# A decoder step with paged attention: ten cache slots instead of eight, another order of softmax work and convolution taps

## What is computed

```python
x  = LN(alpha*x + gate0 * 0.5 * SwiGLU_1(mod0(x)))
q, k, v, ga, gb = split(mod1(x) @ w_in)              # 8 heads of 64, convolution of 512 channels
attn = MoBA(q, k, v, cache_k, cache_v, page_table)   # new tokens: 2048 cached keys in 8 blocks, top 3 blocks
conv = silu(groupnorm(depthwise_conv31(ga * sigmoid(gb))))
x  = LN(alpha*x + gate1 * concat(attn*beta_attn, conv*beta_conv) @ w_out)
x  = LN(alpha*x + gate2 * 0.5 * SwiGLU_2(mod2(x)))
```

## Time and profile before

| | us |
|---|---|
| median of 3 runs (lowest, highest) | 899.49 (899.29, 901.28) |
| the profiled execution | 899.64 |
| its span, first to last instruction | 897.9 |
| TensorE busy | 841.3 (94%) |
| VectorE busy | 457.7 (51%) |
| ScalarE busy | 351.1 (39%) |
| GpSimd busy | 266.8 (30%) |

### The profile page before, as it was taken

One profiled execution on the slowest core, in us unless ns is written; L12 is line 12 of the kernel. 1 busy time (PEld: TensorE's weight loads), 2 busy tenths in 40 slices (PEclk: granted clock), 3 DMA queues, 4 the chain that ended last, 5 costly groups with the idle time before them and its releaser, 6 DMA issues.

```text
span 897.9 us, 17144 instructions
## 1 busy us (share of the span) xinstructions
PE 841.3 (94%) x6798; PEld 745.1 (83%) x6798; DVE 457.7 (51%) x710; ACT 351.1 (39%) x502; POOL 266.8 (30%) x326
## 2 busy tenths in 40 slices
PE   5899999999999999999997779769999999999996
PEld 3789889898899989988764556538899999999996
DVE  1543434343334576745686776844864444444454
ACT  2332333333222467445352314273573333332240
POOL 2020000000010323999999999700200000000121
PEclk9999999999999999999999899999999999999998
DMA  9977777789857444417997999999524444643421
GB/s 300 349 235 255 231 247 243 225 268 303 289 183 244 147 146 145 138 54 236 359 304 269 355 339 362 348 348 290 158 77 153 147 140 141 195 146 134 160 76 58
DMA packets 182130, 197.44 MB, mean 220 GB/s; under 512 B 11908, under 2 KB 163706, under 8 KB 182054
## 3 DMA queue, kind: packets, MB, share of 16 engines
q1 hardware_dynamic: 175149, 190.04, 65.2%
q10 hardware_dynamic: 6624, 6.33, 2.2%
q0 software_dynamic: 288, 0.14, 0.1%
HBM read 193.67 MB, written 3.17 MB: 219 GB/s over the span
## 4 chain that ended last, share of the span: by engine, by line
PE 75%; DVE 8%; SPq 6%; DMA 5%; ACT 3%; issue 3%; POOL 1%; DVEq 0%; ACTq 0%; POOLq 0%
PE bank L1620 19%; PE bank L1621 18%; PE bank L1622 18%; PE bank L1909 5%; SPq L446 3%; PE bank L1587 3%; PE bank L1934 2%; DMA raw<-in_w_ada 2%; DMA raw<-in_ffn_wg 1%; PE bank L1576 1%; DVE kT L1383 1%; PE bank L1652 1%; DMA raw<-in_ffn_wu 1%; DVE wlo L1094 1%; PE bank L1646 1%
## 5 line engine op out<-in xcount | busy, mean ns | idle before, releaser
L1094 DVE TENSOR_TENSOR wlo<-raw,whi 128x2048 fp32r<-128x2048 f32 (+1 forms) x80 | 182.8, 2286 | 235.5 <-ACT whi L716 235.2
L1620 PE MATMUL bank<-mh,whi 128*128 128x320 f32 x816 | 257.5, 316 | 0.0
L1622 PE MATMUL bank<-mh,wlo 128*128 128x320 f32 x816 | 252.2, 309 | 0.0
L1621 PE MATMUL bank<-ml,whi 128*128 128x320 f32 x816 | 252.2, 309 | 0.0
L716 ACT CAST whi<-raw 128x2048 fp32r<-128x2048 f32 (+1 forms) x80 | 148.9, 1861 | 229.3 <-PE bank L1622 155.0
L1620 PEld LDWEIGHTS bank<-mh,whi 128*128 128x128 f32 x816 | 153.3, 188 | 10.4 <-issue 10.3
L1621 PEld LDWEIGHTS bank<-ml,whi 128*128 128x128 f32 x816 | 153.5, 188 | 0.1
L1622 PEld LDWEIGHTS bank<-mh,wlo 128*128 128x128 f32 x816 | 153.3, 188 | 0.0
L1620 PE MATMUL bank<-hh,whi 128*128 128x320 f32 x352 | 111.1, 316 | 0.0
L1621 PE MATMUL bank<-hl,whi 128*128 128x320 f32 x352 | 109.6, 311 | 0.0
L1622 PE MATMUL bank<-hh,wlo 128*128 128x320 f32 x352 | 109.4, 311 | 0.0
(11 more groups left out here) (280 smaller groups left out, 1134.3 us busy)
## 6 DMA issues: line engine op xcount, KB each, us to landing
araw<-in_w_ada SPq DMA_DIRECT2D x28, 1024.0 KB, 5.2
raw<-in_ffn_wg SPq DMA_DIRECT2D x22, 1024.0 KB, 7.1
raw<-in_ffn_wu SPq DMA_DIRECT2D x22, 1024.0 KB, 7.5
raw<-in_ffn_wd SPq DMA_DIRECT2D x16, 1024.0 KB, 5.0
raw<-in_cache_k SPq DMA_DIRECT2D x64, 256.0 KB, 4.5
raw<-in_cache_v SPq DMA_DIRECT2D x60, 256.0 KB, 5.7
raw<-in_w_in SPq DMA_DIRECT2D x10, 1024.0 KB, 5.2
raw<-in_w_ada SPq DMA_DIRECT2D x8, 1024.0 KB, 11.9
```

The costliest lines, as they stand in the source:

```text
L1094: dve.tensor_tensor(wl(slot_w(phase, u))[:, 0:size], landed(phase, u)[:, 0:size], wh(slot_w(phase, u))[:, 0:size].bitcast(F32), ALU.subtra ...
L1620: pe.matmul(bank[:, b, 0:T], wh(slot)[:, c], h_, start=(start and n == 0), stop=False)
L1621: pe.matmul(bank[:, b, 0:T], wh(slot)[:, c], l_, start=False, stop=False)
L1622: ins = pe.matmul(bank[:, b, 0:T], wl(slot)[:, c], h_, start=False, stop=(stop and n == len(parts) - 1))
```

## The change

Parts: (1) ten slots instead of eight, the two new ones, kvm and kvu, laid over mh and over the first chunks of uT; the last fourteen units have a table of their own, KV_LAST, which leaves slots 6 and 7 (kvw) free for W_out after pair 3's keys. Waits are added for what reads mh and uT before, and one before mh is written. uT's chunks are renumbered (v in 4 to 7, k in 8 to 11), so that k stays out of the way. (2) The order of the softmax steps on TensorE and VectorE. (3) The taps: chunk 0's are spread, and six of chunk 3's go from GpSimd to VectorE. (4) ScalarE issues its pages earlier. The diff, cut; first_taps replaces conv_taps where that was called for chunk 0, and blocks_added returns its last instruction:

```diff
@@ -114 @@
 ADA0 = 8
-KVN, KV_RING = 64, 8
+KVN, KV_RING = 64, 10
+KV_LAST = (0, 1, 2, 3, 4, 5, 8, 9, 0, 1, 4, 5, 2, 3)
 ACT_HIGH = (8 + 2, 8 + 5)
+THIRD = 6
@@ -177 @@
 def kv_slot(kvi):
...
-    return kvi % KV_RING if kvi < KVN - 8 else (0, 1, 2, 3, 4, 5, 2, 3)[kvi - KVN + 8]
+    return kvi % KV_RING if kvi < KVN - len(KV_LAST) else KV_LAST[kvi - KVN + len(KV_LAST)]
...
 def kv_turn(kvi):
@@ -256 @@
 yT = sb("yT", [P, NCH, T])
+with ExitStack() as scope:
+    kvm = sb("kvm", [P, UMAX], F32, scope)
@@ -289 @@
     yrow = sb("yrow", [P, 3, D], F32, scope)
+with ExitStack() as scope:
+    kvu = sb("kvu", [P, UMAX], F32, scope)
@@ -344 @@
 def kv_raw(kvi):
...
     k = kv_slot(kvi)
+    if k >= 8:
+        return (kvm, kvu)[k - 8][:, :]
...
 def kT_view(k, half):
@@ -360 @@
 ld_c, c_t, ld_ident = sem("ld_c"), sem("c_t"), sem("ld_ident")
+own_moved, gate_moved, third_prompt, third_sample = sem("own_moved"), sem("gate_moved"), sem("third_prompt"), sem("third_sample")
@@ -564 @@
         sp.wait_ge(w_lo, WIN[0] + WIN[2] - RING + kvi + 1)
+    elif kvi < 9:
+        sp.wait_ge(w_used, WIN[0] + (7, 7, 10, 9, 10)[kvi - RING])
     else:
-        sp.wait_ge(w_used, WIN[0] + (7, 7, 10, 9)[kvi - RING])
+        sp.wait_ge(ps_mm, NH)
+        sp.wait_ge(tok_t, 8)
+        sp.wait_ge(q_ready, 1)
     load_pages(sp, cache, kvi, numbers[8 * (k % 4 // 2) + k % 2:], range(3 if cache == "v" and j < 3 else 4))
-    if kvi == KV_RING + 3:
+    if kvi == KV_RING + 4:
...
         sp.dma_start(o["conv_prompt_new"][0, 0], cout).then_inc(stored_early, 16)
-    if kvi == 4 * KV_RING:
+    if kvi == 32:
...
         for u in range(2):
-            sp.wait_ge(v_used, 16 + 7 + u)
+            sp.wait_ge(kt_ready, 2 * (24 + 7 + u))
...
 for u in range(2, WOUT[2]):
-    load(WOUT, u, cols(i["w_out"], slice(UC * u, UC * u + UC)), NCH * UC, (v_used, 24 + u - 1))
+    load(WOUT, u, cols(i["w_out"], slice(UC * u, UC * u + UC)), NCH * UC, (v_used, 24 + u + 1))
@@ -676 @@
 sam = cbuf[:, c, ST + SEQ:CB].rearrange("p (b k) -> p b k", b=DB)
-for k in range(TAPS):
+if c == 3:
+    pool.wait_ge(third_prompt, THIRD)
+    pool.wait_ge(third_sample, THIRD)
+for k in range(THIRD if c == 3 else 0, TAPS):
@@ -924 @@
 elif c < 12:
-    act.copy(uT[:, c, :], src).then_inc(u_out, 1)
+    act.copy(uT[:, c + 4 if c < 8 else c - 4, :], src).then_inc(u_out, 1)
@@ -970 @@
 def last_page(k, page):
...
     kvi = values_at(j - 1, k)
-    act.wait_ge(kt_ready, 2 * (8 * j + k + 1))
+    cache_b, jb, kb = kv_chunk(kv_before(kvi))
+    act.wait_ge(*((kt_ready, 2 * (8 * jb + kb + 1)) if cache_b == "k" else (v_used, 8 * jb + kb + 1)))
...
     n = 8 * j + k
-    if j and k % 4 == 1:
-        numbers = page_numbers(2 * (j - 1) + k // 4, mybir.EngineType.Activation)
@@ -986 @@
             act.copy(kT_view(k, 1), bank_keys(1)).then_inc(kt_high, 1)
-        if j and k:
-            last_page(k - 1, numbers)
+        if j and k in (0, 3):
+            numbers = page_numbers(2 * (j - 1) + k // 3, mybir.EngineType.Activation)
+        if j and k == 0:
+            last_page(0, numbers)
+        if j and k < 7:
+            last_page(k + 1, numbers)
...
             between[k]()
-    if j:
-        last_page(7, numbers)
...
 def probs(j):
...
-    act.wait_ge(eb_ready, j + 1)
...
     for b2 in range(2):
+        act.wait_ge(eb_ready, 2 * j + b2 + 1)
@@ -1054 @@
 act.wait_ge(gy_ready, c + 1)
+act.wait_ge(v_used, 24 + 1)
@@ -1301 @@
-def conv_taps(first, last):
+def conv_taps(c, first, last, on_prompt, on_sample):
...
+def first_taps(first, last):
+    conv_taps(0, first, last, conv_prompt, conv_sample)
@@ -1365 @@
 sbk, sc = bank[:, 4 + g % 2, :], s_two[j % 2][:, b2, P * n:P * n + 512]
-dve.tensor_reduce(gsum[:, j % 2, b2, n:n + 4], sbk.rearrange("p (m x) -> p x m", x=4), AX, ALU.add)
+ins = dve.tensor_reduce(gsum[:, j % 2, b2, n:n + 4], sbk.rearrange("p (m x) -> p x m", x=4), AX, ALU.add)
+if g == 3:
+    ins.then_inc(gsum_ready, 1)
@@ -1393 @@
                                 con[:, C_OWN + 56 - DT * (2 * j + b2):C_OWN + 56 - DT * (2 * j + b2) + NS], ALU.add)
-    ins.then_inc(gsum_ready, 1)
+    ins.then_inc(own_moved, 1)
...
 def blocks_chosen(j):
...
     s, top = s_two[j % 2], bmax[:, j % 2]
-    dve.wait_ge(gsum_ready, j + 1)
+    dve.wait_ge(own_moved, j + 1)
...
     link(dve.tensor_copy(gate[:, :, :], bank[:, 6, 256:272].rearrange("p (b n) -> p b n", b=2)))
-    dve.tensor_reduce(top[:, 0:1, 8:9], s[:, 0:1, PAST // 2:], AX, ALU.max)
+    dve.tensor_reduce(top[:, 0:1, 8:9], s[:, 0:1, PAST // 2:], AX, ALU.max).then_inc(gate_moved, 1)
@@ -1439 @@
 def first_pair():
...
+    own_added(0)
     score_chunk(0, 3)
-    own_added(0)
...
 def first_bias():
...
-    blocks_added(0, 1)
     bias_ready(0)
+    blocks_added(0, 1).then_inc(eb_ready, 1)
...
 keys_high(0, {0: lambda: prompt_probs(7)})
-keys_high(1, {0: first_pair, 1: lambda: blocks_chosen(0), 3: lambda: blocks_added(0, 0), 4: first_bias, 7: lambda: sums_ready(0)})
-taps = (12, 12, 25, TAPS)
+keys_high(1, {0: first_pair, 1: lambda: blocks_chosen(0), 3: lambda: blocks_added(0, 0), 4: first_bias, 6: lambda: own_added(1), 7: lambda: sums_ready(0)})
...
     if j > 1:
-        keys_high(j)
+        between = {6: lambda: own_added(j)}
+        if j == 2:
+            for n, k in enumerate((1, 3, 5, 7)):
+                between[k] = lambda n=n: first_taps(17 + n, 18 + n)
+        keys_high(j, between)
     score_chunk(j, 3)
-    own_added(j)
     blocks_chosen(j)
-    for b2 in range(2):
-        blocks_added(j, b2)
+    blocks_added(j, 0)
     bias_ready(j)
-    if j == 3:
+    blocks_added(j, 1).then_inc(eb_ready, 1)
+    if j < 3:
+        first_taps(*((12, 17), (21, 25))[j - 1])
+    else:
...
     sums_ready(j)
-    if j < 3:
-        conv_taps(taps[j], taps[j + 1])
+    if j == 1:
+        dve.wait_ge(glu_ready, NCC)
+        conv_taps(3, 0, THIRD, third_prompt, third_sample)
+    if j == 2:
+        first_taps(25, TAPS)
@@ -1812 @@
 def turn_tokens(e):
...
-    at = (8, 4)[e % 2] + 2 * (e // 2)
+    at = (4, 8)[e % 2] + 2 * (e // 2)
@@ -1846 @@
     pe.wait_ge(ps_ready, h)
-q, k = uT[r, h // 2, :], uT[r, 4 + h // 2, :]
+q, k = uT[r, h // 2, :], uT[r, 8 + h // 2, :]
@@ -1937 @@
 def own_scores(j):
...
     pe.wait_ge(gl_out, 2)
+    if j == 1:
+        pe.wait_ge(eb_ready, 1)
...
             ins = pe.matmul(bank[QG * g4:QG * g4 + QG, 6, NS * b2:NS * b2 + NS], qo[:, 2 * j + b2, g4, :],
-                            uT[:, NHP + g4, SEQ:T], start=True, stop=True)
+                            uT[:, 8 + g4, SEQ:T], start=True, stop=True)
...
 def pair_keys(j, between={}):
@@ -1951 @@
     scores(j, k - 1)
-if k == 4 and j != 1:
+if k == (5 if j == 1 else 4):
@@ -1969 @@
 def prob_sum(j):
+    if j == 0:
+        pe.wait_ge(own_moved, 2)
...
 def pair_probs(j):
@@ -1984 @@
 pe.wait_ge(ri_ready, j + 1)
+if j == 0:
+    pe.wait_ge(gate_moved, 2)
@@ -1997 @@
 raw_wait(kvi)
+if k % 2 == 0:
+    pe.wait_ge(pt_evac, 5 * j + k // 2 + 1)
@@ -2009 @@
+pe.wait_ge(pt_evac, 5 * j + 5)
@@ -2030 @@
 pair_keys(0, {0: lambda: prompt_steps(20), 1: lambda: prompt_steps(21), 2: lambda: prompt_steps(22), 3: turn_glu})
-pair_keys(1, {1: lambda: gate_sum(0), 3: lambda: max_swap(0), 6: lambda: prob_sum(0)})
+pair_keys(1, {1: lambda: gate_sum(0), 3: lambda: max_swap(0), 7: lambda: prob_sum(0)})
+gate_sum(1)
 pair_probs(0)
-pe.wait_ge(pt_evac, 5)
-own_scores(1)
...
 def next_pair(j):
...
         pair_keys(j)
-        pe.wait_ge(pt_evac, 5 * j)
-    steps = {0: lambda: gate_sum(j), 2: lambda: max_swap(j), 5: lambda: prob_sum(j)}
+    steps = {4: lambda: max_swap(j), 7: lambda: prob_sum(j)}
+    if j > 1:
+        steps[0] = lambda: gate_sum(j)
     if j == 3:
-        steps[3] = group_means
+        steps[6] = group_means
@@ -2071 @@
-pe.wait_ge(pt_evac, 20)
...
 def conv_half(u, c0, c1):
```

More of the change, by code:

```diff
@@ L1298, in _ @@
             half_gate(2)
-            def conv_taps(first, last):
-                sum_c = yT[:, NCC, :]
+            def conv_taps(c, first, last, on_prompt, on_sample):
+                sum_c = yT[:, NCC + c, :]
                 for k in range(first, last):
-                    sam = cbuf[:, 0, ST + SEQ:CB].rearrange("p (b k) -> p b k", b=DB)[:, :, k:k + DT]
-                    w = dwT[:, NCC * k:NCC * k + 1]
+                    sam = cbuf[:, c, ST + SEQ:CB].rearrange("p (b k) -> p b k", b=DB)[:, :, k:k + DT]
+                    w = dwT[:, NCC * k + c:NCC * k + c + 1]
                     if k == 0:
                         dve.wait_ge(x_ready, 8)
-                        dve.tensor_scalar(sum_c[:, 0:SEQ], cbuf[:, 0, k:k + SEQ], w, par2[:, 0:1], ALU.mult, ALU.add).then_inc(conv_prompt, 1)
-                        dve.tensor_scalar(samples(sum_c), sam, w, par2[:, 0:1], ALU.mult, ALU.add).then_inc(conv_sample, 1)
-                    else:
-                        dve.wait_ge(conv_prompt, k)
-                        dve.scalar_tensor_tensor(sum_c[:, 0:SEQ], cbuf[:, 0, k:k + SEQ], w, sum_c[:, 0:SEQ], ALU.mult, ALU.add).then_inc(conv_prompt, 1)
```

(16 more changed lines are left out.)

## The result

The median went from 900.07 us (899.29 to 901.28, 4 runs) to **894.34 us** (893.76 to 895.61, 4 runs): a ratio of 0.9943, 95% interval 0.9924 to 0.9961, so 5.7 us of gain where 10.4 were forecast. The time lies in the range, at its upper edge. The profiled execution took 895.61 us, its span 893.7.

The account below looks back on a forecast made before the run. The DMA engines' page stream was taken as the bound: 12.9 us missing, less 2.0 emptiness and 0.5 stores, net 10.4. 899.64 - 10.4 - 0.15 = 889.1, stated as 889.0 us; range 884.5 to 894.5.

Parts of the forecast that it names:

- pages bound the stage and the gain is the stream's: Attention stage: the DMA engines' page stream sets the end; filling its short stretches gains 10.4 us net.
- units 24 and 25 out by 476: Pair 0's values: these units go into slots 4 and 5 and issue from 475.6 instead of 482.1 us.
- the readers' schedule: TensorE's attention stages: pair 2's keys at 493.1, pair 1's values at 520.6, pair 2's at 562, pair 3's at 579 us.
- C: Rival, chance 0.06: VectorE becomes the bound, 21 taps among pairs 1 and 2 adding up to 12 us to readers; 896.
- D: Rival, chance 0.04: slower, as with more pages in flight the engines move less after 476 us; 905 in all.
- What stays: Of 12.9 us missing in the stream, 2.0 of emptiness near 481 us and 0.5 for convolution-state stores remain; net 10.4.
- 345 GB/s or more in each stretch from 482 to 595: Sign that the forecast is right: page rate in the attention stage; under 330 with a SyncE wait would show it wrong.
- what stands behind the sixth page follows at a fixed distance: After the last pair's sixth value page: W_out products, last turn and FFN 2 move as a block with unit 61.
- bounded the clock by 0 and 2: TensorE's longer idling before unit 60 could put up to 2 us more work at 1.2 GHz; taken as 0.
- On the path all this costs or gives nothing: New softmax order and taps: covered by the stream; without that cover worth 11 us by pair 2's earlier values.
- not the bound: SyncE's queue from 475.6 us: 115 us of issues, the last could go at 591; engines land that unit near 601.
- GpSimd's last tap: GpSimd loses 6 of 93 taps at 2.26 us and ends near 565 instead of 578.9 us.

Follow-up runs that it names:

- The slot series: Nine, ten and eleven page slots with the new softmax order and taps, beside the kernel before: 897.4, 894.7 and 892.4 us.
- clock_kept: Changed kernel plus twelve matmuls of unused constants on TensorE ahead of value unit 60: 892.94 us, ratio 0.9945 to the kernel before.
- after_again: The changed kernel itself, unchanged, run again beside other versions on one chip: 894.72 us, ratio 0.9947 to the kernel before.
- eleven_slots: Changed kernel with an eleventh slot laid over xT, so the output is not the reference's: 892.40 us, ratio 0.9925 to the kernel before.
- quarters_late: Changed kernel, ScalarE issuing the last pair's fourth value pages, units 60 to 63's behind the group norm's square root: 892.30 us, ratio 0.9931 to the kernel before.
- act_quarters: Changed kernel, ScalarE issuing the last pair's fourth value pages, units 60 to 63's ahead of the group norm's square root: 892.88 us, ratio 0.9927 to the kernel before.
- quarters_late_clock: quarters_late plus six products of constants on TensorE before value unit 60: 893.24 us, ratio 0.9923 to the kernel before.

## Why the prediction was right and wrong

**Right, with numbers:** that pages bound the stage and the gain is the stream's (8.39 us of waiting before unit 60); units 24 and 25 out by 476; the readers' schedule, within 1.2 us up to pair 2's values; no TensorE wait over 1.3 us for a key copy (against C); no loss of rate with more pages in flight, 352 for values and 374 to 385 for keys in the full stretches (against D). Pair 3's values came at 582.6 instead of 579: TensorE waited four times, 3.7 us in all, for pages of pair 2, and ran the eight products of group_means in 3.23 us instead of 2.42, at a granted clock of 0.73.

**The step that failed is "What stays".** I let 2.0 us of emptiness and 0.5 for the stores remain of 12.9. By the same formula on the stretches after: 476-482 70 x 6 / 380 = 1.1; 482-500 54 x 18 / 380 = 2.6; 528-548 6 x 20 / 380 = 0.3; 573-592 27 x 19 / 348 = 1.5: **5.5 us** remain. The edge at 482 cuts through the dry stretch, so by its own edges: the dry stretch, to 483.5, cost 2.6 us where I had left 2.0, and the 4.5 us at part of the rate behind it 1.0 where I had left none. With what little is missing beside them that is 3.7 at the seam, and 3.9 and 3.8 in the two other profiles of the changed kernel. The other miss is a stretch that had been full before, 573 to 592 at 347 GB/s (1.5, none allowed; 1.0 and 0.3 in the other two). I had counted the loss of 482 to 500 as the hole's and took it to go with the hole. That loss goes with a wait at that seam, and the wait stayed: with eleven slots and no dry stretch it is still 336 GB/s. By my own signs, "345 GB/s or more in each stretch from 482 to 595" failed twice, at 326 and 321. So 12.9 - 5.5 = 7.4 were to come; unit 61 came 6.3 us earlier, with the stage starting 0.6 us later in this execution (the prompt's last turning products but one at 419.57, before at 418.96).

The simpler count was at hand in my own text: unit 26 waits for pair 0's first values, "at 481 too". Before it was unit 24. From that wait's end on, two units fewer have to cross: 2 x 2.8 = 5.6 us, and the distance fell by 6.4. By this count emptiness **ahead** of a wait that stays is no gain beyond the units that the new slots take across in it; the 2.8 us of 450 to 476 and the 1.5 of 426 to 450 brought pages forward to stand before the same wait. The slot series fits (2.5 us each, 5.2 from eight to ten with the new readers); that the gain follows this count and no other is argued, not shown.

**A second step failed: "what stands behind the sixth page follows at a fixed distance".** It was 291.4 us before and 293.5 after. I had bounded the clock by 0 and 2 and took 0, "since part of it was slow before"; it cost 1.2. Before, the clock was full to 602 us, with TensorE idle from 599 to 603.4, and four W_out products ran slowly (0.41 to 0.64 us instead of 0.31, until 609.5); now TensorE idled from 588.8 to 597.2, the clock was at the lower level, 1.2 GHz, from about 592 on, and thirteen products, to 605.7, ran slowly. The Trainium skill (TensorE: Matmul & The Clock Gate, "What's actually happening") has idleness bring the lower clock back, the rule that I had weighed; the trace agrees. Of the other 0.9 us nearly all, 0.75, lies in the last 11 us of the kernel, from ScalarE's last activation to the end: 10.2 us before, 10.9 after. ScalarE and the products that turn the output, in before, then in after:

```profile
887.34 1.09 PE L2112 MATMUL bank<-con,yT 128*128 128x128 f32 x8
887.72 0.30 ACT L1079 ACTIVATE rows<-rows,con 128x3 f32<-128x3 f32 x1 [1.69 <-DVE rows L1536]
888.36 1.09 PE L2115 MATMUL bank<-con,yT 128*64 128x128 f32 x16
```

```profile
882.38 1.97 PE L2151 MATMUL bank<-con,yT 128*128 128x128 f32 x8
882.77 0.30 ACT L1097 ACTIVATE rows<-rows,con 128x3 f32<-128x3 f32 x1 [1.69 <-DVE rows L1567]
884.28 1.79 PE L2154 MATMUL bank<-con,yT 128*64 128x128 f32 x16
```

No instruction of that part is changed. What differs is the clock: full before (1.00), 0.54 from 882.3 to 886 now, so the turning products take 1.97 us instead of 1.09 and VectorE waits for them (0.81 us instead of 0.35, and 0.26 more at the next). The part takes 10.1 us in clock_kept, whose turning products all take 1.09 us, and 11.2 in after_again and eleven_slots, where they take 1.97. Why the clock falls there in some executions and not in others is open.

Together, for the profiled execution: unit 61 was forecast at 595.5 and seen at 600.19, 4.7 us late, and the rest is 2.1 longer. That is 6.8, and 895.61 is 6.6 over 889.0.

**"On the path all this costs or gives nothing" was wrong for the softmax steps.** I had it that the stream covers whatever the new order costs or gives, and the new order is a condition of the gain: without it the ten slots bring 1.8 us of distance (123.8) and no time that can be measured. The text had the number that says so (pair 2's values 11 us earlier, slots free only 3.7 and 5 us before they are needed) but did not draw it: 11 is more than 5.

**Smaller misses.** GpSimd's last tap ends at 572.7, not near 565: its taps took longer, 1.12 us instead of 1.02 for the first of the three operations. Nothing waited for it. SyncE's queue was "not the bound" as a total, but a total hides a stretch: at 573 to 592, with four value pages a unit on SyncE at 0.79 us each, the rate was 321 GB/s, and with ScalarE's help 347 to 349. Whether that costs time at unit 61 is open. Two of the prices of rivals do not follow from their own numbers: D's end near 613 is 6.6 us later than before and makes 906, not 905; C's 21 taps at 0.79 us more are 16.6 us, not 12. The forecast rests on neither.

**The Trainium skill's 358 GB/s** (DMA: Bandwidth & Descriptors, "Where 436 GB/s comes from") was rightly not used for keys: this case's trace has 385 GB/s over 24 us, with samples up to 407. The lower figure would have put the forecast nearer to the outcome, but by luck: the time was lost elsewhere.

## What to carry to other kernels

When buffers are added to a ring, find the first wait that the new ring still has, and ask whether its end moves; if it doesn't, each buffer is worth about one transfer (2.5 us measured, 2.8 by the rate) and not the idle time around the wait. Price the slow run-up after a dry spell too (1.0 us here behind 2.6), and a queue by stretches, not by its total. Then test the parts alone: here buffers and earlier readers gave nothing measurable by themselves and 5.7 us together, because each was the other's limit.

## What the runs showed of the hardware

A stream of 256 KB key pages that had run dry did not come back at full rate: 314, 276, 358, 219, 265, 336 GB/s in the changed kernel's first 4.5 us, then 374 and more; with eleven slots, where it never ran dry, there are single samples down to 115 at the same place, so the dry stretch alone is not the reason. The cause was not tested.

Of the versions with ten slots, quarters_late has the lowest median, 892.3 us against 894.9 for the changed kernel on the same chip. By the ratios act_quarters (0.9927), quarters_late (0.9931) and quarters_late_clock (0.9923) can't be told apart, and the intervals of all three overlap that of the changed kernel.
